# Attention value products with the values stationary, in two column halves of the array

## The chip, the cores and the metric

The kernel runs on one core of a Trainium2 chip. The metric is the device time of one execution in microseconds (us). TensorE (PE) does matrix products, VectorE (DVE) and ScalarE (ACT) do element work and copies out of PSUM, GpSimd (POOL) does element work and issues some transfers, SyncE (SP) issues most transfers.

## What is computed

One inference step of a one-layer encoder, float32, 2048 prompt frames and 64 sample frames. Cut to what the change touches:

```
h = rms_norm(x, g);  [qa|ka|va|qb|kb|vb] = h @ w_in;  q, k normalised per head, b with rotary
mixer A, 8 heads:  own chunk of 64 + 8 chunks before;  scores + relative bias
mixer B, 8 query heads, 2 key/value heads:  own chunk + 2 before;  softmax with a sink term
e = exp(scores - max);  out = (e @ v) / sum(e)
x = x + concat(outA, outB) @ w_out
x = x + (silu(causal_conv3(h2 @ w_gate)) * (h2 @ w_up)) @ w_down
```

The sample frames do the same against cached keys and values.

## The kernel before

Four stages follow each other: `project`, `attend`, `combine`, `ffn`, with a barrier of all engines behind each. The change is in `attend`, and in one permutation of the rows of `w_out` on the host.

`attend` works through 17 query tiles of 128 rows: n = 0 is the sample, n = 1 to 16 the prompt. Tile n has 12 units u: u = 0 to 7 are the heads of mixer A, and u = 8 to 11 are pairs of heads of mixer B. A head of A looks at w = min(n, 5) key blocks of 128, a head of B at min(n, 2). From n = 5 on a tile is "whole": five blocks for A, two for B. The first six tiles are written out and the rest is a hardware loop (`Fori`).

Each unit passes through a pipeline over the engines, counted by k = 12n + u. Every engine's order is written by hand:

- PE `scores` (L916, with mask products L907 and L912) into `s_ps[u % 2]`; keys and queries are split into a rounded part and a rest (`q_hi`, `q_lo`).
- DVE adds the bias (L1102) and takes the row maxima (L1109, L1111); ACT takes exp into `prob[u % 2]` and the row sums into `den`.
- PE `transposes` (L933): each 128x128 block of `prob` into `t_ps`, one PSUM tile for all units. ACT copies four blocks to `prob_t[u % 2]` (L1050), DVE the fifth (L1127).
- PE `values` (L949): for each block, `prob_t` is the stationary operand (128 columns) and the head's 64 columns of `v` move; result rows are queries.
- DVE `divide` multiplies with the reciprocal sums (L1144, L1149) into `o`.
- PE `output` (L973): four transposes of `o` for each mixer and tile, and DVE `copy_o` (L1133) to `o_t`, which SP stores.

At step k, PE does scores(k), values(k - 3), transposes(k - 1). `output(n, 0)` comes at u = 11, and `output(n - 1, 1)` at u = 4 after that step's scores.

The next tile's operands come in beside this. SP loads `raw`. ACT at u = 5 of tile n - 1, after exp(5) and the copy of unit 4, copies the keys of tile n (`split_keys`, L1012). POOL then forms the rest of the keys (L858), prepares one piece of the later stages' weights (`weights(n, 0)`, L130 to L143), and forms `q_lo` (L863). PE waits for that (`lo_ok`) before scores(n, 0). POOL then prepares two more pieces and forms the rest for mixer B (`split_b`, L869), for which PE waits at u = 8. In all, POOL prepares 42 pieces in this stage.

Of the kernel before, what the change touches and what calls it, by code (L numbers as in the profile page):

```python
# [637 lines left out]
def attend(nc, q_a, k_a, qk_b, v_all, ka_cache, kb_cache, va_cache, vb_cache, rel_rows, sinks, ident, oT,  # L638
# [4 lines left out]

    TILES = SEQ // P
    UNITS, A_UNITS = 12, HEADS
    FULL = 5
    NEAR = 2 * P
    HALF = FULL * P // 2
    LOOP = FULL + 1  # L660
    KEYS = SEQ + 2 * P
# [4 lines left out]
    CLEARED = 11  # L666
    with ExitStack() as ctx:
        m = Memory(nc, ctx, "attend")
        keys = m.sbuf("keys", [P, NKEY, KEYS], F32R)
        v = m.sbuf("v", [P, TILES + 2, V_FEATURES])  # L670
# [17 lines left out]
        prob_t = [m.sbuf(f"prob_t{i}", [P, FULL * P]) for i in range(2)]  # L688
# [3 lines left out]
        o = m.sbuf("o", [P, 2 * HEADS, HEAD])  # L692
        o_t = [m.sbuf(f"o_t{i}", [P, KD // 2, P]) for i in range(2)]
        s_ps = [m.psum(f"s{i}", [P, 2, 512]) for i in range(2)]
        t_ps = m.psum("t", [P, 1024])
        ot_ps = t_ps[:, 512:1024]
        o_ps = [m.psum(f"o{i}", [P, 512]) for i in range(2)]
# [7 lines left out]
        s_ok, biased, max_ok, exp_ok, t_ok, t_act, t_dve, pv_ok, rden_ok, o_ok = (  # L705
            m.sem(n) for n in ("s_ok", "biased", "max_ok", "exp_ok", "t_ok", "t_act", "t_dve", "pv_ok", "rden_ok", "o_ok"))

        ot_ok, ot_out, o_st = ([m.sem(f"{n}_{x}") for x in "ab"] for n in ("ot_ok", "ot_out", "o_st"))

        def window(n, mixer):  # L710

            if isinstance(n, int) and n == 0:
                return SEQ, 2 * P
            w = FULL if mixer == "a" else 2
            if isinstance(n, int):
                w = min(n, w)
            return (n - w) * P, w * P

        def first_tile(n, mixer):
            return TILES if isinstance(n, int) and n == 0 else n - window(n, mixer)[1] // P  # L720
# [8 lines left out]
        def whole_before(n, u):  # L729

            return 0 if isinstance(n, int) and n < FULL else A_UNITS * (n - FULL) + min(u, A_UNITS)
# [18 lines left out]
        def run(eng, step, last):  # L750

            for n in range(LOOP):
                for u in range(UNITS):
                    step(n, u)
            with eng.Fori(LOOP, TILES + 1) as n:
                for u in range(UNITS):
                    step(n, u)
            last()
# [5 lines left out]
        def _(sp):  # L764
# [7 lines left out]
            def load(n):  # L772
                c, w = (SEQ, DEC) if isinstance(n, int) and n == 0 else ((n - 1) * P, P)
                tile = TILES + 1 if isinstance(n, int) and n == 0 else n - 1
                twice(raw[:, 0:HEADS, 0:w], q_a[:, :, ds(c, w)].rearrange(by_heads, p=HEAD), ld)
                twice(raw[:, HEADS:HEADS + KV_A, 0:w], k_a[:, :, ds(c, w)].rearrange(by_heads, p=HEAD), ld)
                twice(raw[:, HEADS + KV_A:, 0:w], qk_b[PAIRS_B:, :, ds(c, w)].rearrange(by_heads, p=HEAD), ld)
                sp.dma_start(v[0:w, ds(tile, 1), :].rearrange("p a f -> p (a f)"), v_all[ds(c, w), :]).then_inc(ld, 16)

            def load_b(n):  # L780
                c, w = (SEQ, DEC) if isinstance(n, int) and n == 0 else ((n - 1) * P, P)
                twice(raw_b[:, :, 0:w], qk_b[0:PAIRS_B, :, ds(c, w)].rearrange(by_heads, p=HEAD), ld_b)

            def store(n, mixer):

                c, w = (SEQ, DEC) if isinstance(n, int) and n == 0 else ((n - 1) * P, P)
                sp.wait_ge(ot_out[mixer], n + 1)
                half = slice(mixer * KD // 2, (mixer + 1) * KD // 2)
                sp.dma_start(oT[half, :, ds(c, w)].rearrange("k p n -> p k n"), o_t[mixer][:, :, 0:w])\
                    .then_inc(o_st[mixer], 16)  # L790
# [5 lines left out]
            sp.dma_start(v[0:DEC, TILES + 1, :], v_all[SEQ:, :]).then_inc(ld, 16)  # L796
            load_b(0)
            for n in range(LOOP - 1):
                sp.wait_ge(lo_ok, 2 * (n + 1))
                load(n + 1)  # L800
# [6 lines left out]
            with sp.Fori(LOOP - 1, TILES) as n:  # L807
                sp.wait_ge(lo_ok, 2 * (n + 1))
                load(n + 1)
                store(n - 1, 0)  # L810
                sp.wait_ge(lo_b_ok, n + 1)
                load_b(n + 1)
                store(n - 1, 1)
# [8 lines left out]
        def _(pool):  # L822
            pool.dma_start(ident_sb[:], ident).then_inc(const_ld, 16)
            pool.dma_start(v[:, TILES, 0:PAIRS_A * P], va_cache).then_inc(const_ld, 16)
            pool.dma_start(v[:, TILES, PAIRS_A * P:], vb_cache).then_inc(const_ld, 16)
# [3 lines left out]
            for done, (out, value) in enumerate((  # L829
# [3 lines left out]
                    (mask_k[0:1, :, 0:CHUNK], NEG), (mask_k[32:33, :, NEAR - CHUNK:NEAR], NEG), (v[DEC:, TILES + 1, :], 0.0))):  # L833
# [18 lines left out]
            def split(n):  # L852

                if not isinstance(n, int) or n:
                    pool.wait_ge(lo_b_ok, n)
                pool.wait_ge(hi_ok, 2 * n + 1)
                c = SEQ + P if isinstance(n, int) and n == 0 else (n - 1) * P
                nc.gpsimd.tensor_tensor(keys[low, :, ds(c, P)], raw[low, HEADS:, :], keys[low, :, ds(c, P)].bitcast(F32),  # L858
# [27 lines left out]
        def _(pe):  # L886
            def scores(n, u):
# [5 lines left out]
                if not isinstance(n, int) or k > 1:  # L893
                    pe.wait_ge(exp_ok, k - 1)
# [8 lines left out]
                for bank, query, key, first, width in parts:  # L903
# [11 lines left out]
                    for q in (q_hi, q_lo):  # L915
                        last = nc.tensor.matmul(ps[:, bank, 0:width], q[:, query, :], keys[:, key, ds(c + first, width)],  # L916
                                                start=q is q_hi and not begun, stop=q is q_lo, skip_group_check=begun)
                last.then_inc(s_ok, 1)

            def transposes(n, u):  # L920
                k = UNITS * n + u
                pe.wait_ge(exp_ok, k + 1)
                if not isinstance(n, int) or k:
                    pe.wait_ge(t_act, k)
                for j, first in enumerate(prob_blocks(n, u)):
                    if j == FULL - 1:
                        if u == 0:
                            pe.wait_ge(ot_out[0], n)
                        elif u == 3:
                            pe.wait_ge(ot_out[1], n)  # L930
                        else:
                            pe.wait_ge(t_dve, whole_before(n, u))
                    last = nc.tensor.transpose(t_ps[:, j * P:(j + 1) * P], prob[u % 2][:, first:first + P], ident_sb[:])  # L933
                last.then_inc(t_ok, 1)

            def values(n, u):
                k = UNITS * n + u
                pe.wait_ge(t_act, k + 1)
                if is_whole(n, u):
                    pe.wait_ge(t_dve, whole_before(n, u) + 1)  # L940
                if not isinstance(n, int) or k > 1:
                    pe.wait_ge(o_ok, k - 1)
                mixer = "a" if u < A_UNITS else "b"
                tile, w = first_tile(n, mixer), window(n, mixer)[1] // P
                first = u * HEAD if u < A_UNITS else PAIRS_A * P
                for head in range(1 if u < A_UNITS else 2):
                    for j in range(w):
                        src = (head * w + j) * P
# [6 lines left out]
            def output(n, mixer):  # L955

                if mixer:
                    pe.wait_ge(o_ok, UNITS * (n + 1))
                    if isinstance(n, int) and n == TILES:
                        pe.wait_ge(ot_out[0], n + 1)  # L960
                    elif isinstance(n, int) and n + 1 < FULL:
                        pe.wait_ge(ot_out[0], n + 1)
                    else:
                        pe.wait_ge(t_dve, whole_before(n + 1, 3))
                else:
                    pe.wait_ge(o_ok, UNITS * n + A_UNITS)
                    if not isinstance(n, int) or n >= FULL:
                        pe.wait_ge(t_dve, whole_before(n, A_UNITS))
                    elif n:
                        pe.wait_ge(ot_out[1], n)  # L970
                for k in range(KD // 2):
                    heads = slice(HEADS * mixer + 2 * k, HEADS * mixer + 2 * k + 2)
                    last = nc.tensor.transpose(ot_ps[:, k * P:(k + 1) * P],  # L973
                                               o[:, heads, :].rearrange("p a f -> p (a f)"), ident_sb[:])
                last.then_inc(ot_ok[mixer], 1)

            def step(n, u):
# [1704 lines left out]
```

## Time and profile before

| | us |
|---|---|
| median of 3 timed runs | 2562.65 (2561.45 to 2565.75) |
| span of the profiled execution, first to last instruction | 2559.8 |
| median less that span | 2.85 |
| stage `attend`, first score product to the first instruction behind the barrier | 496.3 to 951.7 |

The profiled execution comes with its span alone. What lies around it is taken as the difference to the median of the timed runs. The rows below give starts in us from the span's start. PE is the matrix product and PEld the load of its stationary operand, which overlaps. A float32 product of the program that isn't of the rounded type appears as two instructions each of PEld and PE, so one of the 56 value products of a whole tile is two records; a transpose is one. "128*64" in front of a shape is the part of the array that the instruction uses, rows by columns.

### The profile page before, as it was taken

The page shows a single profiled execution, that of the slowest core. Times are in us where ns is not written, and L with a number is a line of the kernel's source. Part 1 is how long each engine was busy: PE and PEld are TensorE (multiplying, and loading weights), DVE is VectorE, ACT ScalarE, POOL GpSimd, SP SyncE. Part 2 cuts the span into 40 slices and gives each one's busy share as a digit, 9 for nine tenths or more (in the row PEclk, how much of TensorE's full clock was granted, in tenths as well). Part 3 has the DMA queues.
Part 4 walks back from the last instruction along what each step waited for, and adds up shares of the span by engine and source line. Part 5 has one row for each costly group of instructions (what it writes and reads, how often), then busy time and mean ns, then how long its engine had stood idle before and what let it go on. Part 6 is the DMA issues. An engine that isn't in the chain of part 4 may idle for free. (4 is left out here: it accounts for less than half of the span.)

```text
span 2559.8 us, 46391 instructions
## 1 busy us (share of the span) xinstructions
PE 2427.8 (95%) x15365; PEld 2316.4 (90%) x15365; DVE 1727.1 (67%) x3780; ACT 1164.5 (45%) x2658; POOL 992.7 (39%) x1150
## 2 busy tenths in 40 slices
PE   6999999589999989998999999999999999999997
PEld 4888888489999979998899999989999998999997
DVE  7656665466766756767676666767666787676765
ACT  6232322377777653335434444543444454444433
POOL 2888888557878868831220000213000021000001
PEclk9999999789999999999999999999999999999999
DMA  8676776655666759889687666868766677666765
GB/s 260 211 222 208 219 220 194 165 142 156 187 172 166 187 155 347 293 317 336 216 294 220 215 209 221 298 233 310 224 214 216 217 268 271 213 214 214 221 207 179
DMA packets 318205, 577.88 MB, mean 226 GB/s; under 512 B 35490, under 2 KB 167826, under 8 KB 317890
## 3 DMA queue, kind: packets, MB, share of 16 engines
q1 hardware_dynamic: 274576, 424.24, 52.7%
q0 software_dynamic: 39872, 149.75, 18.3%
q10 hardware_dynamic: 3570, 1.52, 0.3%
q8 instruction: 102, 1.67, 0.2%
q14 instruction: 85, 0.70, 0.1%
HBM read 444.88 MB, written 132.10 MB: 225 GB/s over the span
## 5 line engine op out<-in xcount | busy, mean ns | idle before, releaser
L2195 PE MATMUL ffn_x<-carry_big 128*128 128x352 f32 x2508 | 458.5, 324 | 11.4 <-PEq L62 5.7
L2195 PEld LDWEIGHTS ffn_x<-carry_big 128*128 128x128 f32 x2508 | 411.1, 189 | 16.8 <-issue 13.1
L2195 PE MATMUL ffn_z<-ffn_h_hi_S,carry_big 128*128 128x352 f32 x1056 | 278.4, 326 | 20.1 <-DVE carry_big L2340 13.7
L316 PE MATMUL project_z<-project_w_hi,project_h_hi 128*128 128x512 f32 (+3 forms) x680 | 255.6, 376 | 20.5 <-DVE project_w_lo L489 16.3
L316 PE MATMUL project_z<-project_w_hi,project_h_lo 128*128 128x512 f32 (+3 forms) x680 | 252.0, 371 | 0.0
L316 PE MATMUL project_z<-project_w_lo,project_h_hi 128*128 128x512 f32 (+3 forms) x680 | 251.8, 370 | 0.0
L2094 POOL TENSOR_TENSOR carry_x<-carry_x,carry_work 128x352 f32<-128x352 f32 x48 | 52.1, 1086 | 503.9 <-DVE carry_work L2458 445.4
L2088 POOL DMA_DIRECT2D carry_work<-h_sums_scratch x8 | 4.4, 552 | 577.2 <-DVE ffn_y_lo_S L2362 572.8
L2340 DVE TENSOR_TENSOR carry_big<-carry_w_raw,carry_big 128x512 fp32r<-128x512 f32 (+2 forms) x413 | 224.1, 550 | 0.6 <-ACT carry_big L2276 0.4
L949 PE MATMUL attend_o<-attend_v,attend_prob_t 128*128 (+1 forms) x1680 | 213.6, 271 | 0.0
L949 PEld LDWEIGHTS attend_o<-attend_v,attend_prob_t 128*128 128x128 f32 x1680 | 211.6, 194 | 0.6
L2195 PEld LDWEIGHTS ffn_z<-ffn_h_hi_S,carry_big 128*128 128x128 f32 x1056 | 188.3, 189 | 26.3 <-DVE carry_big L2340 26.2
L2276 ACT ACTIVATE carry_big<-carry_w_raw 128x512 fp32r<-128x512 f32 (+2 forms) x413 | 195.4, 500 | 4.7 <-PEq L62 4.5
L2195 PE MATMUL ffn_z<-ffn_h_lo_S,carry_big 128*128 128x352 f32 x528 | 170.5, 323 | 0.0
L316 PEld LDWEIGHTS project_z<-project_w_hi,project_h_hi 128*128 128x128 f32 (+1 forms) x680 | 126.9, 187 | 47.5 <-DVE project_w_lo L489 12.4
L2233 ACT ACTIVATE carry_work<-ffn_x 128x352 f32<-128x352 f32 x138 | 64.0, 464 | 215.3 <-PE ffn_x L2195 215.3
L2195 PE MATMUL ffn_x<-ffn_y_hi_S,carry_big 128*128 128x352 f32 x528 | 152.6, 326 | 9.0 <-DVE carry_x L2433 5.3
L2238 ACT ACTIVATE carry_work<-ffn_x 128x352 f32<-128x352 f32 x138 | 64.1, 465 | 208.0 <-PE ffn_x L2195 208.0
L916 PE MATMUL attend_s<-attend_keys,attend_q_hi 128*128 (+5 forms) x368 | 133.6, 367 | 25.7 <-DVE attend_q_lo L1159 25.7
L2195 PE MATMUL ffn_z<-ffn_y_hi_S,carry_big 128*128 128x352 f32 x528 | 150.6, 323 | 0.0
L316 PEld LDWEIGHTS project_z<-project_w_hi,project_h_lo 128*128 128x128 f32 (+1 forms) x680 | 126.7, 186 | 24.0 <-issue 0.6
L933 PE MATMUL attend_t<-attend_ident,attend_prob 128*128 128x128 f32 x840 | 130.7, 280 | 17.0 <-ACT attend_prob_t L1050 14.0
(264 smaller groups left out, 6498.9 us busy)
## 6 DMA issues: line engine op xcount, KB each, us to landing
carry_big<-t_gu_scratch SPq DMA_DIRECT2D x264, 512.0 KB, 4.1
carry_big<-t_dn_scratch SPq DMA_DIRECT2D x240, 256.0 KB, 3.3
carry_w_raw<-w_gu SPq DMA_DIRECT2D x198, 256.0 KB, 4.2
t_gu_scratch<-project_quads POOLq DMA_DIRECT2D x68, 512.0 KB, 4.5
carry_w_raw<-w_dn SPq DMA_DIRECT2D x180, 128.0 KB, 3.5
project_quads<-w_quads POOLq DMA_DIRECT2D x68, 256.0 KB, 4.2
carry_w_raw<-w_o SPq DMA_DIRECT2D x24, 512.0 KB, 5.9
t_dn_scratch<-attend_quads POOLq DMA_DIRECT2D x22, 512.0 KB, 4.4
```

Of the source, the lines that this page charges most:

```text
L316: last = nc.tensor.matmul(z[c][0:w, 0:width], h[:, k, 0:w], ww[:, k, first:first + width], start=(k == 0 and h is hi and ww is w_hi), stop ...
L916: last = nc.tensor.matmul(ps[:, bank, 0:width], q[:, query, :], keys[:, key, ds(c + first, width)], start=q is q_hi and not begun, stop=q ...
L933: last = nc.tensor.transpose(t_ps[:, j * P:(j + 1) * P], prob[u % 2][:, first:first + P], ident_sb[:])
L949: last = nc.tensor.matmul(o_ps[u % 2][:, head * HEAD:(head + 1) * HEAD], prob_t[u % 2][:, src:src + P], v[:, ds(tile + j, 1), first + head ...
L2088: pool.dma_start(h_source(b, name), src).then_inc(h_ld[H_STAGE[name]], 16)
L2094: nc.gpsimd.tensor_tensor(total, total, part[:], ALU.add).then_inc(done, 1)
L2195: mm = nc.tensor.matmul(bank[:, 0:SUB], weights(c)[:, wp, k, :], (hi, lo)[a][name][:, 1 if short else k, :], start=first and k == 0 and (w ...
L2233: nc.scalar.activation(sum2[g % 2][:], x_ps[g % 2][:, 0:SUB], ACT.Copy).then_inc(sum2_ok, 1)
L2238: nc.scalar.activation(sum3[g % 2][:], x_ps[g % 2][:, 0:SUB], ACT.Copy).then_inc(sum3_ok, 1)
L2276: nc.scalar.activation(weights(c)[:, 0], raw(c), ACT.Copy)\
L2340: nc.vector.tensor_tensor(weights(c)[:, 1], raw(c), weights(c)[:, 0].bitcast(F32), ALU.subtract).then_inc(w_lo_ok, 1)
```

## The change

Six things are changed together:

1. `values` takes two heads at a time (for A, units 2r and 2r + 1, at even steps; for B, each unit as before). Now `v` is stationary (64 columns) and the block of `prob_t` moves (128 columns). Head i writes PSUM partitions 64i to 64i + 63, so the two heads lie in the two column halves of the array. The instructions alternate between heads within each block. The result is already transposed.
2. The reciprocal sums are spread by DVE to 128x128 (`rden_wide`), and one transpose for each pair puts them beside the result (`r_ps`).
3. DVE copies `r_ps` to SBUF (`copy_r`) and multiplies (`divide`) straight into `o_t`. `output`, `copy_o` and `o` are gone. A tile has 8 "products" (4 of A, 4 of B).
4. `t_ps` becomes two tiles, with the fifth block in a third; `prob_t` becomes four tiles; the results of `values` lie in one PSUM bank, not two.
5. All 17 tiles are written out, without a hardware loop. Cached keys use the last two tiles' places in `keys` and `v`.
6. The rows of `w_out` for mixer B are permuted on the host.

```diff
-                        last = nc.tensor.matmul(
-                            o_ps[u % 2][:, head * HEAD:(head + 1) * HEAD], prob_t[u % 2][:, src:src + P],
-                            v[:, ds(tile + j, 1), first + head * HEAD:first + (head + 1) * HEAD].rearrange("p a f -> p (a f)"),
-                            start=(j == 0), stop=(j == w - 1))
-                last.then_inc(pv_ok, 1)
...
+                if c:
+                    pe.wait_ge(o_ok, c)
...
+                for j in range(w):
+                    for i in range(2):
+                        src = prob_t[(k - 1 + i) % 4][:, j * P:(j + 1) * P] if r < PAIRS_A else \
+                            prob_t[k % 4][:, (i * w + j) * P:(i * w + j + 1) * P]
+                        first = (2 * r + i) * HEAD if r < PAIRS_A else PAIRS_A * P + i * HEAD
+                        nc.tensor.matmul(o_ps[i * HEAD:(i + 1) * HEAD, :], v[:, tile + j, first:first + HEAD], src,
+                                         start=(j == 0), stop=(j == w - 1))
+                pe.wait_ge(wide_ok, c + 1)
+                nc.tensor.transpose(r_ps, rden_wide[c % 2][:].rearrange("p a f -> p (a f)"), ident_sb[:]).then_inc(pv_ok, 1)
```

```diff
             for n, u in steps:
+                add_bias(n, u)
+                if n or u > 1:
+                    invert(*before(n, u, 2))
+                maxima(n, u)
+                if product_at(n, u):
+                    copy_r(*product_at(n, u))
+                if n or u:
+                    copy_t(*before(n, u))
+                if product_at(n, u):
+                    divide(*product_at(n, u))
...
+                if u % 2 or u >= A_UNITS:
+                    if c > 1:
+                        dve.wait_ge(pv_ok, c - 1)
+                    dve.wait_ge(rden_ok, k + 1)
+                    nc.vector.tensor_scalar(rden_wide[c % 2][:], rden[c % 2][:].unsqueeze(2).broadcast_to([P, 2, HEAD]), 1.0, None,
+                                            ALU.mult).then_inc(wide_ok, 1)
...
+                nc.vector.tensor_copy(r_sb[:], r_ps).then_inc(r_ok, 1)
...
+                nc.vector.tensor_tensor(o_t[mixer][:, r % PAIRS_A, :], o_ps, r_sb[:], ALU.mult).then_inc(o_ok, 1)
```

`product_at(n, u)` names the product that step (n, u) computes: the one whose last unit is three steps back, or none where that unit is the even one of a pair of A.

## Rows read from the trace of the kernel before

**Rows 1.** The page's head.

```profile
span 2559.8 us, 46391 instructions
```

**Rows 2.** Busy time by stretch: us, then busy us of each engine, PEclk, DMA share, GB/s.

```profile
496.30:606.87 110.57, 96.09 (x712) 90.49 (x713) 67.53 (x224) 79.99 (x234) 58.39 (x44) 0.89 0.56 139
606.87:914.85 307.98, 304.99 (x2640) 298.70 (x2641) 213.80 (x594) 218.67 (x516) 251.34 (x265) 1.00 0.66 177
914.85:951.70 36.85, 31.84 (x274) 30.78 (x271) 22.00 (x61) 19.33 (x49) 26.32 (x34) 0.95 0.42 121
746.75:774.68 27.93, 27.70 (x242) 27.16 (x240) 19.49 (x54) 19.94 (x48) 22.41 (x26) 1.00 0.63 176
```

**Rows 3.** Timeline of PE in whole tile 10: start us, us, engine, line, operation.

```profile
746.75 0.19 PE L912 MATMUL attend_s<-attend_mask_k,attend_mask_q 128*128 128x64 bf16 x1
...
747.45 1.00 PE L949 MATMUL attend_o<-attend_v,attend_prob_t 128*128 x8
748.28 0.60 PE L933 MATMUL attend_t<-attend_ident,attend_prob 128*128 128x128 f32 x4
748.73 0.19 PE L912 MATMUL attend_s<-attend_mask_k,attend_mask_q 128*128 128x64 bf16 x1
...
753.84 1.22 PE L949 MATMUL attend_o<-attend_v,attend_prob_t 128*128 x10
754.90 0.72 PE L933 MATMUL attend_t<-attend_ident,attend_prob 128*128 128x128 f32 x5
755.46 0.19 PE L912 MATMUL attend_s<-attend_mask_k,attend_mask_q 128*128 128x64 bf16 x1
...
756.15 0.60 PE L973 MATMUL attend_t<-attend_ident,attend_o 128*128 128x128 f32 x4
756.59 1.23 PE L949 MATMUL attend_o<-attend_v,attend_prob_t 128*128 x10
...
758.90 1.22 PE L949 MATMUL attend_o<-attend_v,attend_prob_t 128*128 x10
```

**Rows 4.** Timeline of POOL and ACT around the start of tile 10.

```profile
735.17 2.90 POOL L858 TENSOR_TENSOR attend_keys<-attend_raw,attend_keys 64x1280 fp32r<-64x1280 f32 x1 [2.91 <-ACT attend_keys L1012]
...
743.85 2.39 POOL L863 TENSOR_TENSOR attend_q_lo<-attend_raw,attend_q_hi 128x1024 fp32r<-128x1024 f32 x1
...
761.68 1.27 ACT L1012 ACTIVATE attend_keys<-attend_raw 128x1280 f32 x1
```

**Rows 5.** Timeline of PE in `project`: transposes in half the array's rows, and in all of it.

```profile
56.07 0.39 PE L316 MATMUL project_z<-project_w_hi,project_h_lo 128*128 128x512 f32 x1
56.39 0.52 PE L337 MATMUL project_tr<-project_ident,project_stage 64*128 64x64 f32 x5
...
57.06 0.28 PE L316 MATMUL project_z<-project_w_lo,project_h_hi 128*128 128x256 f32 x1
...
59.91 0.71 PE L328 MATMUL project_tr<-project_ident,project_stage 64*128 64x64 f32 x8
...
82.84 0.39 PE L316 MATMUL project_z<-project_w_hi,project_h_lo 128*128 128x512 f32 x1
83.07 1.03 PE L328 MATMUL project_tr<-project_ident,project_stage 128*128 128x128 f32 x8
...
84.06 0.28 PE L316 MATMUL project_z<-project_w_lo,project_h_hi 128*128 128x256 f32 x1
```

**Rows 6.** Loads of 64 and 128 columns, and float32 products with 352 moving columns.

```profile
34.72 0.13 PEld L316 LDWEIGHTS project_z<-project_w_lo,project_h_hi 128*64 128x64 f32 x1
...
L949 PEld LDWEIGHTS attend_o<-attend_v,attend_prob_t 128*128 128x128 f32 x1680 | 211.6, 194 | 0.6
...
1043.86 1.34 PE L1463 MATMUL carry_ms<-carry_work,carry_small 128*128 128x352 f32 x4
```

**Rows 7.** DVE group in tile 10: busy us, mean ns, idle before.

```profile
L1149 DVE TENSOR_TENSOR attend_o<-attend_o,attend_rden 128x128 f32<-128x128 f32 x4 | 1.1, 283 | 0.1
```

**Rows 8.** Waits in tiles 0 to 4: us in total, times, longest.

```profile
PE attend_t L933 <- ACT attend_prob_t L1050: 11.8, 20, 1.4
```

**Rows 9.** Timeline of POOL: its last issue in `attend`.

```profile
943.77 1.03 POOL L143 DMA_DIRECT2D t_dn_scratch<-attend_quads  x1 [0.30 <-POOL attend_quads L138]
```

More of the change, by code:

```diff
@@ L748, in prob_blocks @@
             return [i * HALF + j * P for i in range(2) for j in range(window(n, "b")[1] // P)]
[L750 to L758, printed above, removed]
+        steps = [(n, u) for n in range(TILES + 1) for u in range(UNITS)]
+        ALL = len(steps)
         block = ctx.enter_context(nc.Block())
@@ L806, in _ @@
                     store(n - 1, 1)
[L807 to L813, printed above, removed]
             for n in (TILES - 1, TILES):
@@ L915, in scores @@
                     for q in (q_hi, q_lo):
-                        last = nc.tensor.matmul(ps[:, bank, 0:width], q[:, query, :], keys[:, key, ds(c + first, width)],
+                        last = nc.tensor.matmul(ps[:, bank, 0:width], q[:, query, :], keys[:, key, c + first:c + first + width],
                                                 start=q is q_hi and not begun, stop=q is q_lo, skip_group_check=begun)
@@ L922, in transposes @@
                 pe.wait_ge(exp_ok, k + 1)
-                if not isinstance(n, int) or k:
-                    pe.wait_ge(t_act, k)
+                if k > 1:
+                    pe.wait_ge(t_act, k - 1)
                 for j, first in enumerate(prob_blocks(n, u)):
                     if j == FULL - 1:
[L927 to L933, printed above, removed]
+                        pe.wait_ge(t_dve, whole_before(k))
+                    out = t_fifth[:, 0:P] if j == FULL - 1 else t_ps[k % 2][:, j * P:(j + 1) * P]
+                    last = nc.tensor.transpose(out, prob[u % 2][:, first:first + P], ident_sb[:])
@@ L955, in output @@
[L955 to L975, printed above, removed]
@@ L986, in step @@
                     pe.wait_ge(sink_set, 4)
-                if not (first and u < 3):
-                    values(*before(n, u, 3))
-                if not (first and u < 1):
+                if product_at(n, u):
+                    values(*product_at(n, u))
+                if n or u:
                     transposes(*before(n, u))
-                if u == 11:
-                    output(n, 0)
-            def last():
-                values(TILES, UNITS - 3)
-                transposes(TILES, UNITS - 1)
-                values(TILES, UNITS - 2)
-                values(TILES, UNITS - 1)
-                output(TILES, 1)
@@ L1001, in _ @@
-            pe.wait_ge(k0_ok, 2)
-            run(pe, step, last)
+            values(TILES, PRODUCTS - 3)
+            transposes(TILES, UNITS - 1)
+            values(TILES, PRODUCTS - 2)
+            values(TILES, PRODUCTS - 1)
         @block.scalar
@@ L1077, in _ @@
             for first, count, cache in caches:
-                nc.scalar.activation(keys[:, first:first + count, SEQ:SEQ + P], cache, ACT.Copy).then_inc(k0_hi, 1)
+                nc.scalar.activation(keys[:, first:first + count, CACHE * P:NEW * P], cache, ACT.Copy).then_inc(k0_hi, 1)
             act.wait_ge(zero_ok, 2)
@@ L1082, in _ @@
             split_a(0)
-            for n in range(LOOP):
-                for u in range(UNITS):
-                    step(n, u)
-            with nc.scalar.Fori(LOOP, TILES) as n:
-                for u in range(UNITS):
-                    step(n, u)
-            for u in range(UNITS):
-                step(TILES, u)
+            for n, u in steps:
+                step(n, u)
             copy_t(TILES, UNITS - 1)
@@ L1176, in set_sinks @@
                         .then_inc(sink_set, 1)
-            def step(n, u):
-                first = isinstance(n, int) and n == 0
-                if u == 4 and not first:
-                    copy_o(n - 1, 1)
-                add_bias(n, u)
-                if not (first and u < 2):
-                    invert(*before(n, u, 2))
-                maxima(n, u)
-                if not (first and u < 3):
-                    divide(*before(n, u, 3))
-                if not (first and u < 1):
-                    copy_t(*before(n, u))
-                if u == UNITS - 1:
-                    copy_o(n, 0)
             set_sinks()
@@ L1202, in _ @@
             for i, (head, count, cache) in enumerate(caches):
-                part = keys[HEAD:, head:head + count, SEQ:SEQ + P]
+                part = keys[HEAD:, head:head + count, CACHE * P:NEW * P]
                 dve.wait_ge(k0_hi, i + 1)
```

218 lines of the change are left out of this document (108 added, 110 removed).

## The prediction

> **What bounds the kernel now.** I read the busy time of the stages first, then PE's timeline in one whole tile, then what feeds that tile. The profiled span is 2559.8 us [rows 1], and the median of the timed runs lies 2.85 above it; I sum on the span and carry the 2.85 along. No other stage is touched, so everything is decided between 496.3 and 951.7. In the eleven periods from tile 5 to tile 15 PE is busy for 304.99 of 307.98 us, at full clock (2.4 GHz), with 27.93 us for a tile [rows 2]. The reader should see an engine that is almost never idle; DVE (19.5 of 27.93) and ACT (19.9) have room. Tiles 0 to 4 differ: PE is busy for 96.09 of 110.57 us at a mean granted clock of 0.89 [rows 2].
>
> A busy PE isn't the whole story. Tile 10's first score product starts at 746.75 [rows 3], and the `q_lo` that it needs was ready at 743.85 + 2.39 = 746.24 [rows 4]: 0.51 us earlier. That `q_lo` ends a loop: scores of tile n start, five units later ACT gets to the next keys, POOL needs from 735.17 to 746.24 for keys, one weight piece and `q_lo` [rows 4], and scores of tile n + 1 may start. This loop takes 27.93 - 0.51 = 27.42 us. PE may become faster by 0.51 us a tile before POOL's chain sets the pace; beyond it only what lies inside the loop counts.
>
> **What one value product costs.** A unit of A issues ten records and holds PE from 753.84 to 754.90, 1.06 us; a unit of B eight, 747.45 to 748.28, 0.83 us [rows 3]. So a record costs about 0.106 us. Only 64 columns move in it, while its load of 128 columns lasts 194 ns against 130 ns for one of 64 [rows 6]: the load sets the pace. After the change the load is short, and 128 columns move. Five transposes with 128 moving columns take 754.90 to 755.46, 0.11 us each [rows 3]; four float32 product records with 352 moving columns last 1.34 us together [rows 6], at most 0.335 each, and so at most 0.12 at 128 columns. I use 0.109. One by one, the new records therefore cost what the old ones did. The whole gain rests on whether the two heads' records, in different column halves, run at the same time.
>
> Let b be the time of one block for two heads, four records. Serial, b = 4 x 0.109 = 0.436. Side by side, b = 2 x 0.109 = 0.218, if PE can start a load and a product every 0.055 us. The shortest steady pitch in this trace is (0.71 - 0.52)/3 = 0.063 [rows 5], between transposes whose 64 columns may themselves set it. No row shows two products in different column halves. I take b = 4 x 0.0615 = 0.246, by that nearest row, and keep 0.218 and 0.436 as ends.
>
> The Trainium skill (TensorE: Matmul & The Clock Gate, Part 3: Packing small matmuls) has products in different column groups running concurrently, with starts some 4 ns apart. By it b would be 0.218 and the serial case would not exist. No run here shows it yet.
>
> **Changing the shape of the array.** Each product now leaves the full array and comes back. The trace has this once in clean form, with half the rows instead of half the columns. From the last 512-column product before to the second one after, five small transposes included, 56.07 to 57.06 is 0.99 us; less 5 x 0.063 it is 0.68. Without a change of shape and with eight full transposes it is 82.84 to 84.06, 1.22; less 8 x 0.11 it is 0.34 [rows 5]. So an excursion costs 0.33 us. I take that; the lower end is 0, since column halves may behave otherwise. With the transpose of the sums, each product pays 0.33 + 0.11 = 0.44.
>
> The skill says the same of the drain (TensorEngine Tiling (Array Packing), Key Properties: a change of tiling mode drains TensorE) and gives no price. The trace agrees, with 0.33.
>
> **The sum for PE, whole tile.** Removed: eight output transposes, 2 x (756.59 - 756.15) = 0.88 [rows 3]. A, four pairs: each 2.12 becomes 5b + 0.44. B, four units: each 0.83 becomes 2b + 0.44. From 27.70 busy that makes 18.54 + 28b: 25.4 us at b = 0.246, 24.6 at 0.218, 30.7 at 0.436. PE alone breaks even with 27.93 at b = 0.335.
>
> **The sum for the loop.** From the first scores to the end of unit 5's scores (746.75 to 758.90 [rows 3]) PE now does the values of three units of B and two of A, and one output; ACT's key copy starts at 761.68 [rows 4], behind exp(5), and not behind the values of unit 2. Afterwards three products of B and one pair lie there: -2.12 - 0.44 + (5b + 0.44) + 3(2b + 0.44 - 0.83). DVE at step 5 also spreads the reciprocals between bias and maxima, 0.28 by the nearest 128x128 operation [rows 7]. Together 27.42 - 3.01 + 11b = 27.1 us at b = 0.246. The loop, not PE, sets the tile: 0.8 us less than 27.93, where PE alone would give 2.5. What is late next is `q_lo`: PE should wait for POOL some 1.7 us at each tile's start.
>
> **The rest.** DVE gains eight spreads and eight copies of `r_ps` at 0.28 and turns twelve divides into eight, less two output copies: about 21.5 us of 27.1, and each step's share fits between two scores. Behind the spread queue the maxima, so exp and the transposes; outside the loop path PE's own work covers that. ACT keeps its work. The unrolled loop and the permuted weights I price at nothing: tiles 0 to 5 were already written out, and PE is idle by only 0.23 us a tile. The single result bank makes product c wait for divide(c - 1); in B there are transposes and scores, 0.45 + 0.70, for a copy and a divide (0.57 and two hops). Without that cover it would cost up to 0.3 a unit.
>
> Tiles 0 to 4: the same terms with 2, 1, 2, 3 and 4 blocks for A, 0.11 a record, and minus 0.88 each, give -2.4 us; the second `t_ps` takes away part of 11.8 us of waiting [rows 8], which other links of the chain mostly give back, and some of these tiles run below full clock, where excursions cost more. I take -3, ends 0 and -14. Tail: tile 16 has no successor, so PE's 27.7 - 25.4 = 2.3 counts; POOL's last issue ends at 944.8 [rows 9], 6.9 before the stage's end, so that its landing leaves room for this.
>
> Sum: 11 x 0.8 + 2.3 + 3 = 14.2 us. Span 2545.6; median 2562.65 - 14.2 = 2548.4.
>
> **Rivals.** (a) Cheap excursions and b = 0.218: the loop falls by 3.01 + 1.32 - 2.40 = 1.9 to 25.5, PE needs 22.0. 11 x 2.4 + 5.7 + 5 = 37 faster, 2525. For it: the price of 0.33 comes from row halves. (b) The column halves don't overlap: the change doesn't do what it says. PE needs 30.7, that is 11 x 2.8 + 3.0 + 7 in the early tiles (13 more, half of it covered by 14.5 idle) = 41 slower, 2603. With excursions at nothing it is 18.54 + 12.2 - 2.6 = 28.1, 2565. It decides from b = 0.335. For it: float32 products come in two records of one head in a row, so the overlap must be found across heads; nothing in the trace shows an overlap. (c) Overlap, but the loop with the added spread and hops eats it: within 5 us, 2560. For it: only 0.8 us a tile is left by my own sum, and one more hop of 0.3 in the loop takes a third.
>
> **How the numbers follow.** A difference of 0.2%, 5 us, is about what a measurement of this kernel can tell from none. Overlap in some degree 0.79: near my sum 0.47 (2537 to 2557), near (a) 0.19, (c) 0.11, overlap and yet slower 0.02. Serial 0.21: 0.03 within 5 us, 0.18 slower. That is faster 0.66, same 0.14, slower 0.20. The likeliest case's own range is 2537 to 2557; to leave out no more than 2 in 10 it goes from 2522, just below (a), to 2580, halfway into (b).
>
> **What would show it.** Right: records of value products starting in pairs, a block for two heads in 0.22 to 0.25 us; 0.3 us around each product; scores of each whole tile waiting for `q_lo` on POOL for 1 to 2 us; starts of tiles 27.1 apart. Wrong: a block in 0.44 and a period near 30; or excursions far below 0.3 and a period near 25.5, with POOL hardly idle; or PE waiting for `divide` or for exp inside the tiles, which would put DVE's order in POOL's place. The prediction fails most easily in the price of an excursion, which counts four times in the loop and eight times on PE.

## The result, and the profile after

The changed kernel takes 2616.67 us (median of 4 runs, 2611.41 to 2623.48), against 2562.05 for the kernel before (2561.09 to 2565.75): a ratio of 1.0216, 95% interval 1.0198 to 1.0235. The forecast was 2548, in 2522 to 2580. It was wrong in sign: to "slower" it had given 0.20, and to what came, an overlap and yet slower, 0.02.

First the page's head and the busy time by stretch. The stretches run between the first score products of tiles 0, 5 and 16, and to the first product of `combine`; they answer to [rows 2].

```profile
span 2616.8 us, 44863 instructions
...
494.77:624.49 129.72, 100.58 (x713) 76.32 (x714) 96.28 (x270) 78.54 (x232) 61.34 (x48) 0.83 0.49 123
624.49:974.41 349.92, 285.40 (x2642) 235.60 (x2641) 299.75 (x704) 216.38 (x516) 250.20 (x265) 0.98 0.58 155
974.41:1020.08 45.67, 29.75 (x273) 24.12 (x270) 28.96 (x80) 22.94 (x55) 27.41 (x34) 0.84 0.48 148
```

The eleven whole tiles take 349.92 us, 41.9 more than in [rows 2]; the early tiles 19.2 more; the tail to `combine` 1.8 more (before, that product started at 958.76). The rest of the program is 6 us shorter. In the whole tiles PE's busy time fell by 19.6 us, where the forecast had 25. Another engine grew: DVE went from 213.8 to 299.75 us. Eight spreads and eight copies a tile at 0.28 would be 49 us; less four divides and two output copies a tile that is about 22. It gained 86.

PE's granted clock changed too. In the eleven whole tiles of the kernel before it was 1.00 (2.4 GHz). In the changed kernel, where PE is idle for some 6 us of each, five of the eleven show 0.94 to 0.97, so part of their time was at 1.2 GHz. One of them, with columns as above:

```profile
752.67:785.78 33.11, 26.73 (x243) 22.06 (x240) 27.77 (x65) 19.74 (x48) 22.96 (x25) 0.95 0.57 150
```

The six at 1.00 take 31.5 us in the mean, the kernel before 28.0. So of the 3.8 us that a tile lost, 3.5 are there at full clock as well; the clock isn't the cause, though what it adds wasn't measured by itself.

The group of instructions that write the spread (ns: shortest, median, longest):

```profile
L1078 DVE TENSOR_SCALAR attend_rden_wide<-attend_rden x136: 226/433/3498, 499.7 to 1005.8; 128x128 f32<-128x128 f32 x136
```

One size, one form, and durations from 226 to 3498 ns. The timeline of DVE at three of them, and of POOL at the same places:

```profile
766.75 1.85 DVE L1078 TENSOR_SCALAR attend_rden_wide<-attend_rden 128x128 f32<-128x128 f32 x1
...
772.49 2.64 DVE L1078 TENSOR_SCALAR attend_rden_wide<-attend_rden 128x128 f32<-128x128 f32 x1
775.05 0.81 DVE L1062 TENSOR_REDUCE attend_nmax<-attend_s 128x1 f32<-128x640 f32 x1
...
779.98 3.34 DVE L1078 TENSOR_SCALAR attend_rden_wide<-attend_rden 128x128 f32<-128x128 f32 x1
783.24 0.68 DVE L1064 TENSOR_REDUCE attend_nmax<-attend_s 128x2 f32<-128x514 f32 x1
...
784.15 0.29 DVE L1101 TENSOR_TENSOR attend_o_t<-attend_o,attend_r_sb 128x128 f32<-128x128 f32 x1
```

```profile
766.16 2.37 POOL L863 TENSOR_TENSOR attend_q_lo<-attend_raw_b,attend_q_hi 128x1024 fp32r<-128x1024 f32 x1 [3.63 <-ACT attend_q_hi L984]
772.14 2.90 POOL L852 TENSOR_TENSOR attend_keys<-attend_raw,attend_keys 64x1280 fp32r<-64x1280 f32 x1 [3.61 <-ACT attend_keys L972]
...
779.25 1.03 POOL L143 DMA_DIRECT2D t_gu_scratch<-attend_quads  x1 [0.30 <-POOL attend_quads L138]
780.27 0.56 POOL L118 DMA_DIRECT2D attend_quads<-w_quads  x1
780.83 2.40 POOL L857 TENSOR_TENSOR attend_q_lo<-attend_raw,attend_q_hi 128x1024 fp32r<-128x1024 f32 x1
```

Each long spread ends just behind the end of one GpSimd operation: 42 of the 43 that last over 1 us by 0.1 us or less, one by 0.18 (768.60 behind 768.53, 775.13 behind 775.04, 783.32 behind 783.23). The last one began while GpSimd was still issuing transfers and lasted until `q_lo` was done. GpSimd's own durations are as before: 2.90 and 2.40 against 2.90 and 2.39 in [rows 4]. What the 136 spreads take above 227 ns each is 7.6 us a whole tile and 109 us in all. Only this instruction of DVE is affected; the copies and divides around it, which read PSUM, stay at 0.27 to 0.29. The kernel before has the same operation, `tensor_scalar`, in its divide (L1144, 128x64), with its input in PSUM: 273 to 286 ns in all of 136 cases, beside the same GpSimd work.

The Trainium skill has the rule (SBUF — State Buffer, section Who interferes with whom): VectorE's second pair of SBUF ports is GpSimd's, the one that comes second stands still for the other's whole instruction, and `tensor_scalar` is among the forms that can ask for it, while `tensor_reduce` never does. Its lock fits the ends above; I had not weighed it.

What the standstill does to the others, by the waits between 626 and 970, which is nearly all of the whole tiles (us in total, times, longest; in the kernel before the first of them is 66.9 in its whole tiles):

```profile
ACT attend_prob L995 <- DVE attend_nmax L1062: 100.7, 65, 2.7
...
POOL attend_keys L852 <- ACT attend_keys L972: 39.7, 11, 3.6
...
PE attend_t L923 <- ACT attend_prob L995: 35.9, 45, 1.1
...
PE attend_o L940 <- DVE attend_o_t L1101: 25.1, 23, 2.3
```

And PE's timeline up to the first scores of the next tile:

```profile
779.39 0.28 PE L910 MATMUL attend_s<-attend_keys,attend_q_lo 128*128 128x256 f32 x1
779.60 1.31 PE L940 MATMUL attend_o<-attend_prob_t,attend_v 128*64 128x128 f32 x20
780.84 0.33 PE L943 MATMUL attend_o<-attend_ident,attend_rden_wide 128*128 128x128 f32 x1
781.01 0.60 PE L923 MATMUL attend_t<-attend_ident,attend_prob 128*128 128x128 f32 x4
...
784.59 0.66 PE L940 MATMUL attend_o<-attend_prob_t,attend_v 128*64 128x128 f32 x8 [2.27 <-DVE attend_o_t L1101]
...
785.78 0.19 PE L906 MATMUL attend_s<-attend_mask_k,attend_mask_q 128*128 128x64 bf16 x1
```

Read the two together. The spread is free at 783.32; behind it DVE still owes the maxima, a copy of `r_ps` and the divide, and PE may not write the single result bank before that divide (784.15). So the product at 784.59 waited 2.27 us, and the scores of the next tile follow at 785.78.

The same rows price the products. Twenty records go from 779.60 to 780.84, 1.24 us; ten pairs at 0.109 are 1.09. The excursion is the rest: 0.15 there, 0.09 ahead (0.21 between the starts at 779.39 and 779.60, where scores follow each other in 0.12) and 0.06 behind (0.17, where transposes have 0.11): 0.30.

### The profile page after: what moved, and what is told of

The parts are those of the page before. It is cut to its first block and busy times, and to the rows that moved or that the text cites. A ratio compares the mean times of both kernels' runs of the same rounds, so it can differ in the third digit from the quotient of the medians.

```text
span 2616.8 us, 44863 instructions
## 1 busy us (share of the span) xinstructions
PE 2411.6 (92%) x15365; PEld 2233.7 (85%) x15365; DVE 1858.5 (71%) x3950; ACT 1161.3 (44%) x2658; POOL 992.4 (38%) x1150
## 5 line engine op out<-in xcount | busy, mean ns | idle before, releaser
L2137 PEld LDWEIGHTS ffn_x<-carry_big 128*128 128x128 f32 x2508 | 412.7, 190 | 17.2 <-issue 13.5
L940 PE MATMUL attend_o<-attend_prob_t,attend_v 128*64 128x128 f32 x1680 | 128.0, 290 | 37.0 <-DVE attend_o_t L1101 36.3
L910 PE MATMUL attend_s<-attend_keys,attend_q_hi 128*128 128x256 f32 (+4 forms) x368 | 137.5, 378 | 24.7 <-DVE attend_q_lo L1110 24.7
L995 ACT ACTIVATE attend_prob<-attend_s,attend_nmax 128x640 f32<-128x640 f32 (+4 forms) x136 | 96.8, 712 | 139.5 <-DVE attend_nmax L1062 134.9
L923 PEld LDWEIGHTS attend_t<-attend_ident,attend_prob 128*128 128x128 f32 x744 | 88.3, 148 | 79.0 <-ACT attend_prob L995 70.7
```

The source lines that it names most:

```text
L923: last = nc.tensor.transpose(out, prob[u % 2][:, first:first + P], ident_sb[:])
L940: nc.tensor.matmul(o_ps[i * HEAD:(i + 1) * HEAD, :], v[:, tile + j, first:first + HEAD], src, start=(j == 0), stop=(j == w - 1))
L995: nc.scalar.activation(sb, ps, ACT.Exp, bias=nmax[u % 2][:, 0:1], accum_out=den[u % 4][:, 0:1])\
L2137: mm = nc.tensor.matmul(bank[:, 0:SUB], weights(c)[:, wp, k, :], (hi, lo)[a][name][:, 1 if short else k, :], start=first and k == 0 and (w ...
```

## The experiments

I split each whole tile's period at three places of GpSimd's loop: S to K, from the tile's first scores to ACT's copy of the next keys; K to Q, from there to the end of `q_lo`; Q to S, from there to the next tile's first scores. Typical tiles; the period is the mean from tile 5 to 16; time is the median. In the changed kernel S to K lies between 16.2 and 18.1, 17.0 in the mean; the means of e10, e11 and e12 are 13.0, 17.2 and 17.8.

| kernel | time | period | S to K | K to Q | Q to S |
|---|---|---|---|---|---|
| before | 2562.05 | 28.00 | 14.93 | 12.50 | 0.50 |
| changed | 2616.67 | 31.81 | 16.33 | 12.50 | 2.55 |
| e1 spread on ACT | 2559.81 | 27.93 | 15.26 | 12.50 | 0.06 |
| e2 spread by reciprocal | 2563.2 | 28.27 | 15.54 | 12.50 | 0.06 |
| e3 before, plus spread | 2646.97 | 33.59 | 16.0 to 20.5 | 12.49 | 3.3 to 4.9 |
| e4 before, unrolled | 2562.52 | 28.19 | 15.15 | 12.50 | 0.47 |
| e5 spread by reduce | 2556.14 | 27.72 | 14.98 | 12.50 | 0.06 |
| e6 e5 and early keys | 2530.58 | 25.98 | 12.78 | 12.58 | 0.57 |
| e7 e6, heads in turn | 2551.93 | 27.75 | 12.79 | 12.68 | 2.27 |
| e8 before, early keys | 2565.0 | 28.07 | 13.30 | 12.50 | 2.25 |
| e9 e6, two SBUF inputs | 2574.58 | 28.54 | 12.89 | 12.88 | 2.61 |
| e10 changed, early keys | 2571.21 | 28.47 | 12.76 | 12.81 | 2.55 |
| e11 changed, product 4 by reduce | 2593.41 | 30.00 | 17.34 | 12.50 | 0.23 |
| e12 changed, product 2 by reduce | 2600.25 | 30.39 | 17.5 to 18.0 | 12.50 | 0.06 |

The kernel before, run beside them, took 2561.5, 2561.9, 2560.6 and 2559.9 us (e1 to e4, e5 to e8, e9 and e10, e11 and e12).

**e1, e2: the spread without `tensor_scalar`.** e1 gives it to ScalarE; e2 has DVE's reciprocal write it, with a broadcast input, in place of reciprocal and spread.

```diff
+                    nc.scalar.activation(rden_wide[c % 2][:], rden[c % 2][:].unsqueeze(2).broadcast_to([P, 2, HEAD]), ACT.Copy)\
+                        .then_inc(wide_ok, 1)
...
-                    nc.vector.tensor_scalar(rden_wide[c % 2][:], rden[c % 2][:].unsqueeze(2).broadcast_to([P, 2, HEAD]), 1.0, None,
-                                            ALU.mult).then_inc(wide_ok, 1)
```

```diff
+                if u < A_UNITS:
+                    nc.vector.reciprocal(rden_wide[c % 2][:, u % 2, :], den[u % 4][:, 0:1].broadcast_to([P, HEAD])).then_inc(rden_ok, 1)
+                else:
+                    nc.vector.reciprocal(rden_wide[c % 2][:], den[u % 4][:, 0:2].unsqueeze(2).broadcast_to([P, 2, HEAD])).then_inc(rden_ok, 1)
```

> The changed kernel, with the spread of the reciprocal sums to 128x128 done by ScalarE behind its copy of the transposes, and no longer by VectorE. Theory A (VectorE's spread, SBUF to SBUF, stands still while GpSimd works, and all that is queued behind it on VectorE is late): the changed kernel's 136 spreads took 140 us in all, 227 ns each where undisturbed, so about 109 us are lost there. Without them the time falls to 2540 to 2556 us, near the blind sum. Theory B (VectorE's two new copies per product, or the single result bank that makes a product wait for the divide before it, set the pace): the copies and the bank stay, so it stays above 2590 us.

> The changed kernel, with the spread folded into VectorE's reciprocal: it reads the sums broadcast and writes 64 or 128 columns at once; no second instruction. Theory A: if the reciprocal, which in both traces never varied (144 to 168 ns), doesn't stand still for GpSimd, the time is that of e1 within 5 us; if it does, durations above 1 us show in its row and the time stays above 2590. Theory B: above 2590 with durations that don't vary.

Measured: 2559.81 (ratio to before 0.9992, 0.9981 to 1.0002) and 2563.2 (1.0006, 0.9997 to 1.0016). ACT's spread lasts 299 to 338 ns:

```profile
L1018 ACT ACTIVATE attend_rden_wide<-attend_rden x136: 299/307/338, 501.2 to 946.5; 128x128 f32<-128x128 f32 x136
```

The reciprocals last 539 to 555 ns for 64 columns and 941 to 956 for 128, none longer. e2 costs DVE 0.56 us more a product than small reciprocals and an undisturbed spread (for A, 2 x 0.54 - 2 x 0.15 - 0.23) and is still 53 us below the changed kernel. So theory A holds, but e1 is 4 us above the range that I had expected: the whole loss goes with that one instruction, though the forecast gain doesn't come back with it.

**e3, e4: the kernel before, with one part added.** e3 adds the spread alone, its result unused; e4 only writes the tiles out.

```diff
+                if u % 2 or u >= A_UNITS:
+                    dve.wait_ge(rden_ok, k + 1)
+                    nc.vector.tensor_scalar(rden_wide[:], rden[u % 2][:, 0:1].unsqueeze(2).broadcast_to([P, 2, HEAD]), 1.0, None,
+                                            ALU.mult).then_inc(wide_ok, 1)
```

```diff
-            with nc.scalar.Fori(LOOP, TILES) as n:
+            for n in range(LOOP, TILES):
```

> The kernel before, with one added VectorE instruction per future product behind the reciprocal: the same spread, SBUF to SBUF, 128x128, to a tile that nobody reads. Nothing else of the change. Theory A: this one instruction alone makes the kernel before slower by 15 to 60 us, with durations up to 3.4 us that end together with GpSimd's operations. Theory B: 136 times 0.23 us lie in VectorE's idle time (8 us of 28 in each tile), so the time is 2562 within 5 us.

> The kernel before, with all 17 query tiles written out and no hardware loop. Theories A and B: no difference, 2562 within 5 us. Theory C (code loading of the unrolled tiles costs the engines time): slower by 10 us or more.

```profile
L1125 DVE TENSOR_SCALAR attend_rden_wide<-attend_rden x136: 226/393/3556, 500.6 to 1029.8; 128x128 f32<-128x128 f32 x136
```

e3: 2646.97, ratio 1.0324 (1.0307 to 1.0342). One instruction that nobody waits for costs 85 us, more than the 15 to 60 that I expected and more than the whole change lost: DVE works in order, and its maxima, copies and divides stand behind it. e4: 0.9996 (0.9979 to 1.0013); unrolling costs nothing that can be told.

**e5: the same place, the same size, another form.** The maximum over an axis of length one is a copy.

```diff
-                    nc.vector.tensor_scalar(rden_wide[c % 2][:], rden[c % 2][:].unsqueeze(2).broadcast_to([P, 2, HEAD]), 1.0, None,
-                                            ALU.mult).then_inc(wide_ok, 1)
+                    nc.vector.tensor_reduce(rden_wide[c % 2][:], rden[c % 2][:].unsqueeze(2).broadcast_to([P, 2, HEAD]).unsqueeze(3),
+                                            AX.X, ALU.max).then_inc(wide_ok, 1)
```

> The changed kernel, with the spread still one VectorE instruction, SBUF to SBUF, 128x128 and at the same place in its order, but written as a maximum over an axis of length one instead of a multiplication by a constant. Theory A1 (it is this operation's way of using the SBUF ports that makes it stand still for GpSimd, not its place or its data): every spread takes 0.22 to 0.30 us without outliers, and the time is 2546 to 2556: tiles then start every 27.1 us, with scores waiting for GpSimd's q_lo (0.06 us between them). Theory A2 (any SBUF-to-SBUF instruction of VectorE of this size stands still for GpSimd): outliers above 1 us again, and above 2600.

Measured: 2556.14, ratio 0.9984 (0.9973 to 0.9996). The spread, and PE at the start of a tile:

```profile
L1078 DVE TENSOR_REDUCE attend_rden_wide<-attend_rden x136: 285/285/289, 501.0 to 942.3; 128x128 f32<-128x128 f32 x136
```

```profile
746.98 0.20 PE L906 MATMUL attend_s<-attend_mask_k,attend_mask_q 128*128 128x64 bf16 x1 [1.14 <-POOL attend_q_lo L857]
```

285 ns is the price that I had assumed, and here it is constant, though 108 of the 136 spreads began while a GpSimd element operation was running: 58 ns slower than an undisturbed `tensor_scalar`, and 60 us faster in the kernel. With it the scores of every whole tile follow `q_lo` by 0.06 us, and PE stands idle 1.14 us for it: GpSimd's loop sets the pace, as forecast. But S to K is 14.98, where it was 14.93, and not less by 0.6, as my sum has it at b = 0.218.

**e6, e8: is it the loop?** ACT copies the next keys one unit earlier, in e6 on top of e5, in e8 in the kernel before.

```diff
-                if u == 5 and prefetch:
+                if u == 4 and prefetch:
```

> As e5, and ScalarE copies the next tile's keys one unit earlier (u = 4 instead of 5), so GpSimd's chain to q_lo starts some 2.3 us earlier. Theory L (in e1 and e5 the loop over ScalarE's key copy and GpSimd's 12.5 us to q_lo sets a tile's time): the period falls by 1.5 to 2.3 us to about 25.2, where TensorE (24.3) and GpSimd's own 24.6 bound it: 2523 to 2538 us. Theory M (the waits inside a tile, for exp, for the divide and for the copy, set it): the period stays within 0.5 us of e5's and q_lo is early instead.

> The kernel before, with ScalarE's key copy one unit earlier. TensorE is busy for 27.70 of 27.93 us there and q_lo is 0.51 us early already, so both theories: no difference, 2562 within 5 us. It is the control for e6.

e6: 2530.58 (2524.07 to 2532.76), ratio 0.9872 (0.9844 to 0.99), in the range of theory L. This beats both kernels. e8: 1.0016 (1.0002 to 1.003), no gain: there `q_lo` becomes ready 2.25 us early, and PE itself is full for 28 us. So the early keys are worth 25.6 us only where PE has become cheaper. Tile 10 in e6 (columns as in [rows 2]):

```profile
757.85:783.78 25.93, 24.83 (x242) 20.92 (x240) 20.91 (x66) 19.64 (x47) 21.66 (x24) 1.00 0.70 191
```

PE is busy for 24.83 us where it was 27.70 [rows 2].

**e7: do the column halves overlap?** e6 with one head's records all ahead of the other's.

```diff
-                for j in range(w):
-                    for i in range(2):
+                for i in range(2):
+                    for j in range(w):
```

> As e6, but each product does all blocks of the first head and then all of the second, so no two neighbouring records lie in different column halves except where the heads change. If the overlap of the column halves is worth what the starts in the trace say (a block of two heads 0.218 us, serial 0.436), TensorE needs 28 x 0.2 = 5 to 6 us more for a whole tile and the time is 50 to 70 us above e6. If the order doesn't matter, it is that of e6.

```profile
702.77 2.02 PE L940 MATMUL attend_o<-attend_prob_t,attend_v 128*64 128x128 f32 x20
704.72 0.33 PE L943 MATMUL attend_o<-attend_ident,attend_rden_wide 128*128 128x128 f32 x1
```

Measured: 2551.93, 21.4 us above e6, where 50 to 70 were expected. A product of twenty records takes 2.02 us instead of 1.31; one of eight stays at 0.66. So the order of issue matters, which shows that the halves overlap; but the other order isn't serial. The second head's records start at 703.48 while the first's still run. In serial order twenty records at 0.109 would take 2.18; here the next instruction starts after 1.95. In the tile from 711.93 to 739.67 PE is busy for 27.20 us, 2.4 more than in e6, and idle for 0.54, where it was 1.10; the mean period grew by 1.77.

**e9: another form that could be held.** e6 with the spread as a product of two SBUF tiles.

```diff
+                    nc.vector.tensor_tensor(rden_wide[c % 2][:], ones[:], rden[c % 2][:].unsqueeze(2).broadcast_to([P, 2, HEAD]),
+                                            ALU.mult).then_inc(wide_ok, 1)
```

> The kernel of e6 (2530.6 us) with the spread of the reciprocal sums once more in another form: a tensor_tensor that multiplies a tile of ones by the broadcast reciprocals, both read from SBUF, same size and place. What is to be told apart: whether VectorE's instruction stands still for GpSimd because of the form (tensor_scalar alone) or because it reads SBUF beside GpSimd. If any VectorE instruction with two SBUF inputs is held as the tensor_scalar was, some 8 in 88 of the whole tiles' spreads last over 1 us, up to about 3.5, and the time is 2560 to 2600 us. If only the tensor_scalar is held, the spreads last 0.2 to 0.4 us each with none over 1 us, and the time is 2526 to 2537 us. The second is my guess at 0.4 only: the Trainium skill, page SBUF — State Buffer, section Who interferes with whom, lists the tensor_tensor with two SBUF inputs among those that contend.

Measured: 2574.58, ratio 1.0053 (1.0034 to 1.0071): held as well, against my guess. 22 of the 88 spreads of the whole tiles last over 1 us. DVE's timeline and POOL's:

```profile
751.67 0.29 DVE L1080 TENSOR_TENSOR attend_rden_wide<-attend_ones,attend_rden 128x128 f32<-128x128 f32 x1
...
752.97 2.30 DVE L1080 TENSOR_TENSOR attend_rden_wide<-attend_ones,attend_rden 128x128 f32<-128x128 f32 x1
```

```profile
750.83 1.04 POOL L143 DMA_DIRECT2D t_gu_scratch<-attend_quads  x1 [0.30 <-POOL attend_quads L138]
751.85 0.56 POOL L118 DMA_DIRECT2D attend_quads<-w_quads  x1
752.76 2.36 POOL L859 TENSOR_TENSOR attend_q_lo<-attend_raw,attend_q_hi 128x1024 fp32r<-128x1024 f32 x1 [0.35 <-ACT attend_q_hi L980]
```

It ends 0.15 us behind `q_lo`. The one at 751.67 ran its 0.29 us while GpSimd issued a transfer; the `tensor_scalar` at 779.98 above began in such an issue and didn't come free. What is held here has both inputs in SBUF; the divide, also a `tensor_tensor` but with one input in PSUM, stays at 0.28.

**e10: early keys in the changed kernel.** The edit of e6, the `tensor_scalar` kept.

> The changed kernel, its tensor_scalar spread kept, with ScalarE's copy of the keys' scores moved one unit earlier, as in e6. In e6 this was worth 25.6 us over e5, where the scores of each tile waited for GpSimd's q_lo to within 0.06 us. In the changed kernel q_lo is ready 2.55 us before the scores start, so GpSimd's loop sets nothing there. If the spread's standstills alone set its tile period: no gain, 2617 us within 8 either way, q_lo early by 4 us or more. If the early keys help by themselves, it comes to about 2590 us.

Measured: 2571.21 (2566.2 to 2575.96), 45 us faster, neither the 2617 of the one case nor the 2590 of the other. My theory fell. I had read the 2.55 us between `q_lo` and the scores as slack. The table says otherwise: in typical tiles S to K became 3.6 us shorter and Q to S stayed at 2.55, where slack would have grown. (In the kernel before it did grow, from 0.50 to 2.25 in e8; there it was slack.) DVE isn't free until `q_lo` ends, because the spread stands still for it; then come maxima, copy, divide, and PE's product. The loop is closed through the standstill instead of through the semaphore. In e10:

```profile
780.60 2.25 DVE L1078 TENSOR_SCALAR attend_rden_wide<-attend_rden 128x128 f32<-128x128 f32 x1
```

```profile
784.12 0.66 PE L940 MATMUL attend_o<-attend_prob_t,attend_v 128*64 128x128 f32 x8 [1.17 <-DVE attend_o_t L1101]
```

**e11, e12: one spread of the eight.** Product 4's was held for `q_lo`, product 2's for `keys`.

```diff
+                    if c % PRODUCTS == 4:
+                        nc.vector.tensor_reduce(rden_wide[c % 2][:], rden[c % 2][:].unsqueeze(2).broadcast_to([P, 2, HEAD]).unsqueeze(3),
+                                                AX.X, ALU.max).then_inc(wide_ok, 1)
+                    else:
```

> The changed kernel, with one spread of the eight of each tile (product 4, the one that in the trace of the changed kernel stood still for 3.0 to 3.3 us until GpSimd's q_lo ended) formed by tensor_reduce. Theory: GpSimd's loop still sets the period, and this standstill lies in it: the spread comes free 0.1 us after q_lo ends and the scores follow 2.45 us behind, where e5 had 0.06 us between q_lo and the scores. Then this one instruction is worth 11 tiles x 2.5 us and some in tiles 4, 5 and 16: period 29, q_lo to scores 0.06 to 0.5 us, time 2583 to 2593 us. Rival (each standstill simply adds its length to a busy VectorE): 3.1 of 7.6 us of excess a tile, so 3.1/7.6 of the 64 us between the changed kernel and e5 is 25 us: nearly the same here, told apart by e12.

> The changed kernel, with another single spread of the eight (product 2, which stood still for 2.4 us until GpSimd's keys ended) formed by tensor_reduce. Theory of the loop: this standstill lies beside GpSimd's own work from keys to q_lo, which the loop waits for anyway, so it is worth nothing: time 2611 to 2621 us, period 31 to 32, q_lo to scores 2.55 us as before. Rival (each standstill adds its length to VectorE): 2.4/7.6 of 64 us is 20 us, so 2597 us.

e11: 2593.41, 23 us faster, at the upper end of both expectations. Q to S fell from 2.55 to 0.23, as the closed loop says; but S to K didn't shrink (17.2 in the mean, before 17.0), so that the period is 30.0 and not 29. e12: 2600.25, 16 us faster where I expected nothing. Without the halt at `keys` DVE was further on when `q_lo` ran, and product 5's spread was caught:

```profile
742.52 2.16 DVE L1082 TENSOR_SCALAR attend_rden_wide<-attend_rden 128x128 f32<-128x128 f32 x1
```

```profile
744.65 0.20 PE L906 MATMUL attend_s<-attend_mask_k,attend_mask_q 128*128 128x64 bf16 x1 [1.15 <-POOL attend_q_lo L857]
```

That one lies behind the product which the scores wait for, so Q to S is 0.06, and its delay appears in S to K (17.8 in the mean). The excess of the spreads fell from 7.6 us a tile to 5.35 (e11) and 4.2 (e12). So both expectations were too simple: a halt that is removed brings another spread under the same GpSimd operation. The rival, length alone, gave 25 and 20 us and came near in both. It fails in e10. There the early keys change no instruction of DVE, and yet the excess fell too, to 4.4 us a tile, 3.2 less. By the rival's rate (64 us for 7.6) that is 27 us, and e10 gained 45; e12, with 3.3 less, gained 16. So no one price for a us of standstill fits. Where in the loop it falls matters as well, and how much of each halt lies there depends on the alignment; that was not predicted.

## Why the prediction was wrong

**The failed step** is DVE's, in "The rest": the spread priced at 0.28 and each step's share fitting between two scores. The price came from the nearest 128x128 operation [rows 7], alike in size, type and engine. But that one reads PSUM, and the spread reads and writes SBUF beside GpSimd, which is at work for 22 of 28 us. It took 0.23 to 3.5 us. e5 changes nothing else and is 60.5 us below the changed kernel: more than the whole loss of 54.6. So my share for each step didn't fit between two scores, and the sign of being wrong that I had named, PE waiting for `divide` and for exp inside the tiles, is the one that came.

**Right.** Overlap of the column halves: b is 2 x 0.109 = 0.218, the lower end, where I took 0.246; rival (b) is out. The two records of a pair start at 779.60 and 779.61, as the Trainium skill had it (TensorE: Matmul & The Clock Gate, Part 3: Packing small matmuls). The excursion: 0.30 against 0.33; the price from row halves [rows 5] carried over. Unrolling at nothing: e4. The loop over GpSimd, with the scores behind it once the spread is mended: e5's 0.06 us, and 12.50 from keys to `q_lo` as before. With the two measured prices PE alone would need 18.54 + 6.10 - 8 x 0.03 = 24.4 us; e6 shows 24.83.

**Wrong besides, seen once the spread is mended.** e5 gives 2556.1 and not 2548.4, which is rival (c): the loop eats the gain. Of S to K I had taken off PE's work (3.01 - 11b). The trace has ACT's exp waiting for DVE's maxima in that part, and it came to 14.98 against 14.93. I had counted a spread there once, at step 5. It stands in the first step too: in e5's tile at 746.98 the maxima start 0.81 us behind the bias, in the kernel before 0.46 (748.11 less 747.65), and the first exp starts 2.64 us behind the first scores, before 2.22. From there to K it is 12.32, before 12.71. So the first step alone takes 0.42 of the 0.6; how the rest divides was not separated. The early tiles, forecast at -3, are +2.2 in e5 and +19.2 in the changed kernel.

**The single bank.** I priced it at up to 0.3 a unit if uncovered. In the changed kernel it is a path by which a late DVE stops PE, for 25.1 us between 626 and 970; with a steady spread (e6) it is 0.33 at a time and 3.8 us in all. What two banks would give was not tried.

**The sum of the change.** Its idea is worth 31.5 us (e6 against before) once DVE's new instruction is of a form that isn't held, and the keys start one unit earlier.

## What to carry to other kernels

Before pricing an instruction by a like one, ask where its operands lie and which engine works beside it: a small VectorE instruction from SBUF to SBUF, next to long GpSimd operations, can cost up to what is left of GpSimd's work, and delay all that VectorE has queued behind it. Which form it has decides that: here `tensor_scalar` and the `tensor_tensor` with two SBUF inputs were held, `tensor_reduce` and the reciprocal at the same place were not. In the trace its sign is one group whose longest is many times its shortest, ending with another engine's instruction. And a gap is slack only if it grows when what stands ahead of it is made earlier; one that keeps its length closes a loop.

## What the runs showed of the hardware

- A `tensor_scalar` of 128 elements a partition, float32, SBUF to SBUF: 226 ns alone, up to 3556 ns beside GpSimd. It was held by GpSimd's element operations, and some that began in a transfer issue stood as well (779.98). The `tensor_tensor` with both inputs in SBUF: 291 ns alone, up to 3472.
- Not held: `tensor_reduce` 285 to 289 ns (136 cases in e5), ACT's copy 299 to 338 (136), reciprocals 539 to 555 (136) and 941 to 956 (68), `tensor_scalar` from PSUM 273 to 286 (136, the kernel before).
- Two column halves, float32: twenty records in 1.24 us to the next start when they alternate. Issued one head behind the other they still overlap in part: twenty in 1.95, eight in no more time than alternating.
- From the full array to column halves and back, with one transpose behind: 0.30 us.
